# A transformer layer on one core: attention's high parts move from VectorE to ScalarE and GpSimd, and the fixed SBUF places move to a top on 128 bytes

## The chip, the cores and the metric

The kernel runs on one core of a Trainium2 chip. The metric is the device time of one launch in microseconds. TensorE multiplies, VectorE (DVE), ScalarE (ACT) and GpSimd (POOL) do the element work, and SyncE (SP) issues most transfers.

## What is computed

One layer over 2048 frames of width 1024, in fp32:

```
h = x @ w_in                                   # one projection for both head groups
o_gdn = gated_delta_rule(...)                  # 4 heads, chunks of 64 frames
q_nope,q_rope = rms_norm(c_q) @ w_uq ; k_nope,v = rms_norm(c_kv) @ w_ukv ; rotary on q_rope, k_rope
for each block of queries, head by head:       # 4 heads, 128 + 64 wide, v 128 wide
    s = (q_nope k_nope^T + q_rope k_rope^T) * scale, later chunks masked
    o = softmax(s) v
x = layer_norm(alpha x + concat(o_gdn, o_mla) @ w_out)
x = layer_norm(alpha x + (silu(gate) * up) @ w_down)
out = x + sigmoid(x @ w_ple_gate) * (p @ w_ple)
```

## The kernel before

Every fp32 product is made of three matmuls in a fast fp32 format. An operand x is split into a high part (x rounded by a copy into that format) and a low part (x minus the high part), and low x high, high x low and high x high are added in PSUM. So every operand needs one copy and one subtraction before TensorE can use it.

The program is a row of stages: input projection (tiles in_), latents (lat_), delta rule (dr_), attention (at_), output projection with norm (op_), the feed-forward's first half (ff_), its second half with norm (fd_), and the embedding (em_). Each stage is one block of five engine programs that are written out in full; each engine runs its own in order, with semaphores between them, and a barrier of all engines stands between two stages. op, fd and em share one product routine (class TokenProduct, its matmuls at L2451 to L2453): the moving operand of a matmul is the weight (512 columns), the stationary one the activation (128 columns).

**Where tiles lie.** A Scope places a stage's tiles one behind the other from the first free byte of a partition, 16,512 (129 x 128); each start is rounded up to 32 bytes. An Early places tiles at a fixed distance below a top, so that a stage can load them while the stage before still runs. A partition's usable end is 229,368. All distances below the top are multiples of 128, so a fixed tile's remainder modulo 128 is that of the top. Before, the top is 229,344, with remainder 96. Fixed are: attention's inputs of head 0, which serve all even heads (q_hi0, q_lo0, k_hi0, k_lo0, v_hi0, v_lo0, qr0), the rotary keys of all heads (kr, kr_hi), the raw buffers of op, ff, fd and em, and the weights' high and low parts in fd and em. Placed by a Scope are attention's inputs of odd heads (remainder 0), its prob (0), pT_hi and pT_lo (64), op's weights and activations (both 32), fd's activations (32: an identity of 512 bytes and four small tiles, together 160 bytes, lie ahead of them) and em's activations (0).

**Attention.** Queries are cut into 8 blocks of 256 per head, in the order j = 7, 0, 6, 1, 5, 2, 4, 3; block j has j+1 pairs of key tiles, so a head has 36 pairs. For every pair TensorE transposes four 128x128 tiles of probabilities (L1702), ScalarE rounds them (pT_hi, L1751), VectorE subtracts (pT_lo, L1814), and TensorE multiplies them with v (L1716 to L1718). The tiles are turned two pairs ahead of their use (AHEAD = 2, three buffers). In the same pairs the scores of the block three places on are made: five matmuls for each group of 512 keys (L1685 to L1689), a row maximum on VectorE (L1782), an exp on ScalarE (L1738); at a block's end VectorE makes factors from maxima and sums (gap L1792, scale L1808) and GpSimd multiplies the probabilities by them (L1651). All of this is listed by one generator, steps(), and each engine walks the list in its own order.

**Pieces.** While head h is worked on, head h+1's q, k, rotary q and v are loaded and split, in 16 pieces of 512 columns (kind = m % 4: q, k, rotary q, v), spread over the pairs 2 to 20 of the head. Head 3 has no next head and no pieces. SyncE loads a piece into one of four raw slots (`load`, L1856 to L1861), as soon as the low part of the piece four before it is done. VectorE makes the high part (split_highs: L1828, and L1825 and L1826 for rotary q) behind the maxima of that pair. GpSimd makes the low part (`low`: L1662, L1659) and counts split_low.

**Start.** GpSimd clears an identity and writes its diagonal. TensorE waits for it before its first score, though only the transposes read it.

Of the kernel before, what the change touches and what calls it, by code (L numbers as in the profile page):

```python
# [28 lines left out]
P = 128  # L29
# [55 lines left out]
class Early:  # L85
# [4 lines left out]
        self.nc, self.stage, self.sems = nc, stage, []  # L90

    def sb(self, name, shape, below_top, dt=F32):
        top = self.nc.sbuf_usable_end // 32 * 32
        return self.nc.alloc_sbuf_tensor_at(f"{self.stage}_{name}", shape, dt, offset=top - below_top)

    def sem(self, name):
# [59 lines left out]
def reached(eng, sem, count):  # L156

    if not (isinstance(count, int) and count <= 0):
        eng.wait_ge(sem, count)
# [1378 lines left out]
def attention(nc, made, mixT, at, op, w_out, mixed):  # L1538
# [20 lines left out]
    with ExitStack() as ctx:  # L1559
# [6 lines left out]
        ident = s.sb("ident", [P, P])  # L1566
        raw = s.sb("raw", [P, RAW, NTOK])
        qr_hi = s.sb("qr_hi", [P, NTOK], F32R)
        prob = [s.sb(f"prob{n}", [P, 2, (SEQ, SEQ // 2)[n % 2]]) for n in range(4)]
        negm = s.sb("negm", [P, 4, 2, 4])  # L1570
        sums = s.sb("sums", [P, 4, 2, 4])
# [12 lines left out]

        const_sem = s.sem("consts")
        raw_loaded = [s.sem(f"raw_loaded{n}") for n in range(RAW)]
        split_high, split_low = s.sem("split_high"), s.sem("split_low")
        score_done = s.sem("score_done")
        diag_done = s.sem("diag_done")
        max_done = s.sem("max_done")  # L1590
# [48 lines left out]
        @block.gpsimd  # L1639
        def _(pool):  # L1640
            def scaling(n):
                pool.wait_ge(scale_done, n + 1)
                g, ops = groups[n], []
                for tile in range(2):
                    if g > 1:
                        view = keys_of(n, tile, 0, NTOK * (g - 1)).rearrange("p (g n) -> p g n", n=NTOK)
                        ops.append((view, scale[:, n % 4, tile, 0:g - 1].unsqueeze(2).broadcast_to([P, g - 1, NTOK])))
                    w = widths(blocks[n][1], tile)[-1]
                    ops.append((keys_of(n, tile, g - 1, w), scale[:, n % 4, tile, g - 1:g].broadcast_to([P, w])))
                for view, by in ops:  # L1650
                    last = pool.tensor_tensor(view, view, by, ALU.mult)  # L1651
                last.then_inc(scaled, 1)

            def low(h, m):
                count, slot, kind, ts = piece(h, m)
                b, src = h % 2, raw[:, slot]
                pool.wait_ge(split_high, count + 1)
                if kind == 2:
                    pool.tensor_tensor(qr[b][0:ROPE, ts], src[0:ROPE], qr_hi[0:ROPE].bitcast(F32), ALU.subtract).then_inc(split_low, 1)  # L1659
                else:  # L1660
                    high, to = ((q_hi, q_lo), (k_hi, k_lo), None, (v_hi, v_lo))[kind]
                    pool.tensor_tensor(to[b][:, ts], src, high[b][:, ts].bitcast(F32), ALU.subtract).then_inc(split_low, 1)  # L1662

            pool.memset(ident[:], 0.0).then_inc(const_sem, 1)
            pool.wait_ge(const_sem, 1)
            pool.affine_select(out=ident[:], in_=ident[:], compare_op=ALU.not_equal, fill=1.0, base=0, pattern=[[-1, P]],
                               channel_multiplier=1).then_inc(const_sem, 1)
            for n in range(LOOK):
                scaling(n)
            for n, p, turns, now, ends, whole, left, pieces in steps():  # L1670
                if whole is not None:
                    scaling(whole)
                for h, m in pieces:
                    low(h, m)

        @block.tensor
        def _(pe):
# [12 lines left out]

            def turn(n, p):
                j, k = blocks[n][1], pair0[n] + p
                if p == 0:
                    pe.wait_ge(scaled, n + 1)
                reached(pe, lo_done, k + 1 - T_RING)
                for kt in range(2):
                    for tile in range(2):
                        if p == j and kt > tile:
                            continue
                        to = QB * kt + P * (tile if p < j or kt == 0 else 0)  # L1700
                        src = prob[n % 4][:, tile, P * (2 * p + kt):P * (2 * p + kt) + P]
                        last = pe.transpose(pT_ps[:, k % T_RING, to:to + P], src, ident[:])  # L1702
                last.then_inc(turned, 1)
# [14 lines left out]
                    last = pe.matmul(acc, v_hi[b][:, vs], pT_hi[:, r, ps], start=False, stop=diag)  # L1718
                last.then_inc(pv_done, 1)

            pe.wait_ge(const_sem, 2)
            for n in range(LOOK):
                for group in score_groups(n):
                    scores(*group)
# [8 lines left out]
        def _(act):  # L1733
            def exps(n, tile, g, w, G, _):
                if tile == 0 and g == 0 and n >= 4:
                    act.wait_ge(turned, pair0[n - 3])
                act.wait_ge(max_done, G + 1)
                act.activation(keys_of(n, tile, g, w), score_ps[:, G % S_RING, 0:w], ACT.Exp,  # L1738
                               bias=negm[:, n % 4, tile, g:g + 1], accum_out=sums[:, n % 4, tile, g:g + 1]).then_inc(exp_done, 1)
# [13 lines left out]
            def out_copy(n):  # L1753
                act.wait_ge(pv_done, pair0[n + 1])
                reached(act, stored[n % 2], 16 * (n // 2))
                act.activation(out[:, n % 2], acc_ps[:, n % ACCS, 0:QB], ACT.Copy).then_inc(out_done, 1)

            act.preload_act_table(ACT.Exp)
            for n in range(LOOK):
                for group in score_groups(n):  # L1760
# [2 lines left out]
            for n, p, turns, now, ends, whole, left, pieces in steps():  # L1763
                if left is not None:
                    out_copy(left)
                for n1, p1 in turns:
                    high(n1, p1)
                for group in now:
                    exps(*group)
                if ends is not None:  # L1770
                    factors(ends)
            out_copy(N - 1)
# [2 lines left out]
        def _(dve):  # L1775
# [38 lines left out]
                dve.tensor_tensor(pT_lo[:, r, 0:w], pT_ps[:, r, 0:w], pT_hi[:, r, 0:w].bitcast(F32),  # L1814
                                  ALU.subtract).then_inc(lo_done, 1)

            def split_highs(h, m):
                count, slot, kind, ts = piece(h, m)
                b, src = h % 2, raw[:, slot]
                if h > 1 and m == 0:  # L1820
                    dve.wait_ge(pv_done, pair0[NB * (h - 1)])
                dve.wait_ge(raw_loaded[slot], sum(32 if j % 4 == 2 else 16 for j in range(slot, count + 1, RAW)))
                if kind == 2:
                    reached(dve, split_low, count + 1 - 4)
                    dve.tensor_copy(qr_hi[:], src)  # L1825
                    dve.tensor_copy(qr[b][ROPE:, ts], src[ROPE:]).then_inc(split_high, 1)  # L1826
                else:
                    dve.tensor_copy((q_hi, k_hi, None, v_hi)[kind][b][:, ts], src).then_inc(split_high, 1)  # L1828

            for n in range(LOOK):  # L1830
                for group in score_groups(n):
                    maximum(*group)
# [2 lines left out]
            for n, p, turns, now, ends, whole, left, pieces in steps():  # L1835
                for n1, p1 in turns:
                    low(n1, p1)
                if whole is not None:
                    scales(whole)
                for group in now:  # L1840
                    maximum(*group)
                for h, m in pieces:
                    split_highs(h, m)
                if ends is not None:
                    gaps(ends)

# [1022 lines left out]
```

## Time and profile before

| | |
|---|---|
| median of 3 timed runs | 3357.72 us (3351.21 to 3359.09) |
| the profiled execution | 3339.58 us, span 3338.0 us |
| mean granted TensorE clock | 0.965 |
| TensorE matmuls busy | 3081.1 us, 92% |
| VectorE, ScalarE, GpSimd busy | 1648.7, 1056.6, 1057.2 us |
| attention, first score to last matmul | 1061.8 to 1459.1 us |

A matmul is pipelined: its shown length overlaps the next one's. The pace of a stream is the distance from one start to the next. The clock column of the windows is a share of the full 2.4 GHz; the granted clock has the two levels 1.2 and 2.4 GHz, so 0.88 means that 24% of the stretch ran at 1.2 GHz.

### The profile page before, as it was taken

The page shows a single profiled execution, that of the slowest core. Times are in us where ns is not written, and L with a number is a line of the kernel's source. Part 1 is how long each engine was busy: PE and PEld are TensorE (multiplying, and loading weights), DVE is VectorE, ACT ScalarE, POOL GpSimd, SP SyncE. Part 2 cuts the span into 40 slices and gives each one's busy share as a digit, 9 for nine tenths or more (in the row PEclk, how much of TensorE's full clock was granted, in tenths as well). Part 3 has the DMA queues.
Part 4 walks back from the last instruction along what each step waited for, and adds up shares of the span by engine and source line. Part 5 has one row for each costly group of instructions (what it writes and reads, how often), then busy time and mean ns, then how long its engine had stood idle before and what let it go on. Part 6 is the DMA issues. An engine that isn't in the chain of part 4 may idle for free. (4 is left out here: it accounts for less than half of the span.)

```text
span 3338.0 us, 44243 instructions
## 1 busy us (share of the span) xinstructions
PE 3081.1 (92%) x15074; PEld 2541.3 (76%) x15074; DVE 1648.7 (49%) x2773; ACT 1056.6 (32%) x2363; POOL 1057.2 (32%) x1184
## 2 busy tenths in 40 slices
PE   7999997869997889989979999899998999999898
PEld 5888885658886777878758888788887788887776
DVE  3654004536665777656585555865555433233433
ACT  2111014335554444542243333433333211111321
POOL 2322241066665555410073333543331000000122
PEclk9999998979998989999989999999999999999999
DMA  3211115422324211125723222232223433233433
GB/s 137 87 75 75 75 57 183 143 75 75 82 63 106 61 50 54 67 76 181 239 69 115 94 75 80 71 117 94 76 79 111 136 97 96 90 96 122 148 121 99
DMA packets 284412, 329.17 MB, mean 99 GB/s; under 512 B 33280, under 2 KB 224640, under 8 KB 279936
## 3 DMA queue, kind: packets, MB, share of 16 engines
q1 hardware_dynamic: 238632, 265.84, 25.0%
q0 software_dynamic: 12384, 45.09, 3.8%
q10 hardware_dynamic: 33280, 16.78, 1.8%
q8 instruction: 62, 1.02, 0.1%
q14 instruction: 54, 0.44, 0.0%
HBM read 210.73 MB, written 116.92 MB: 98 GB/s over the span
## 5 line engine op out<-in xcount | busy, mean ns | idle before, releaser
L2061 PE MATMUL ff_bank<-ff_x_hi,ff_w_lo 128*128 128x512 f32 x1240 | 488.3, 394 | 32.8 <-DVE ff_w_lo L2241 22.0
L2062 PE MATMUL ff_bank<-ff_x_lo,ff_w_hi 128*128 128x512 f32 x1240 | 487.4, 393 | 0.0
L2063 PE MATMUL ff_bank<-ff_x_hi,ff_w_hi 128*128 128x512 f32 x1240 | 486.9, 393 | 0.0
L2044 POOL TENSOR_TENSOR ff_w_sum<-ff_w_raw 128x512 f32<-128x512 f32 x210 | 299.6, 1436 | 496.9 <-DVE ff_w_lo L2241 438.0
L2061 PEld LDWEIGHTS ff_bank<-ff_x_hi,ff_w_lo 128*128 128x128 f32 x1240 | 235.7, 190 | 85.2 <-DVE ff_w_lo L2241 25.0
L296 PE MATMUL in_h_ps<-in_x_hi,in_w_lo 128*128 128x512 f32 x704 | 276.6, 393 | 25.0 <-POOL in_w_lo L252 25.0
L2451 PE MATMUL fd_acc<-fd_w_hi,fd_a_lo 128*128 128x512 f32 x704 | 280.1, 398 | 10.8 <-DVE fd_a_lo L2435 10.7
L2452 PE MATMUL fd_acc<-fd_w_lo,fd_a_hi 128*128 128x512 f32 x704 | 278.3, 395 | 0.0
L2453 PE MATMUL fd_acc<-fd_w_hi,fd_a_hi 128*128 128x512 f32 x704 | 278.1, 395 | 0.0
L297 PE MATMUL in_h_ps<-in_x_lo,in_w_hi 128*128 128x512 f32 x704 | 276.1, 392 | 0.0
L298 PE MATMUL in_h_ps<-in_x_hi,in_w_hi 128*128 128x512 f32 x704 | 276.0, 392 | 0.0
L2063 PEld LDWEIGHTS ff_bank<-ff_x_hi,ff_w_hi 128*128 128x128 f32 x1240 | 235.8, 190 | 49.7
L2062 PEld LDWEIGHTS ff_bank<-ff_x_lo,ff_w_hi 128*128 128x128 f32 x1240 | 235.8, 190 | 49.0
L2140 ACT ACTIVATE ff_w_hi<-ff_w_sum 128x512 fp32r<-128x512 f32 x210 | 132.5, 631 | 288.3 <-PE ff_bank L2063 267.1
L2435 DVE TENSOR_TENSOR fd_a_lo<-fd_a_raw,fd_a_hi 128x256 fp32r<-128x256 f32 x176 | 74.5, 423 | 286.2 <-ACT fd_a_hi L2425 286.2
L2425 ACT ACTIVATE fd_a_hi<-fd_a_raw 128x256 fp32r<-128x256 f32 x176 | 73.4, 417 | 361.4 <-PE fd_acc L2453 356.5
L1651 POOL TENSOR_TENSOR at_prob<-at_prob,at_scale 128x1536 f32<-128x1536 f32 (+4 forms) x112 | 137.8, 1261 | 149.3 <-DVE at_scale L1808 141.1
L296 PEld LDWEIGHTS in_h_ps<-in_x_hi,in_w_lo 128*128 128x128 f32 x704 | 133.4, 189 | 53.8 <-issue 16.8
L2530 POOL DMA_DIRECT2D scratch_x<-fd_w_raw x16 | 8.5, 534 | 511.8 <-DVE fd_w_raw L2631 511.8
L2451 PEld LDWEIGHTS fd_acc<-fd_w_hi,fd_a_lo 128*128 128x128 f32 x704 | 132.2, 188 | 45.1 <-DVE fd_w_lo L2432 10.8
L2453 PEld LDWEIGHTS fd_acc<-fd_w_hi,fd_a_hi 128*128 128x128 f32 x704 | 132.2, 188 | 32.7
L2452 PEld LDWEIGHTS fd_acc<-fd_w_lo,fd_a_hi 128*128 128x128 f32 x704 | 132.3, 188 | 31.4
(380 smaller groups left out, 6582.6 us busy)
## 6 DMA issues: line engine op xcount, KB each, us to landing
ff_w_raw<-w_gate_up SPq DMA_DIRECT2D x44, 1024.0 KB, 5.1
scratch_hT<-in_out SPq DMA_DIRECT2D x22, 1024.0 KB, 3.9
fd_a_raw<-scratch_hid SPq DMA_DIRECT2D x176, 128.0 KB, 2.1
dr_qkv<-scratch_hT SPq DMA_DIRECT2D x16, 768.0 KB, 5.1
in_w_raw<-w_in POOLq DMA_DIRECT2D x22, 512.0 KB, 3.9
scratch_hid<-ff_first SPq DMA_DIRECT2D x44, 256.0 KB, 2.3
scratch_hid<-ff_second SPq DMA_DIRECT2D x44, 256.0 KB, 2.3
fd_w_raw<-w_down SPq DMA_DIRECT2D x22, 512.0 KB, 5.3
```

Source lines behind the costliest of these rows:

```text
L296: pe.matmul(acc, w_lo[:, b, ws], x_hi[:, k, ts], start=(k == 0), stop=False)
L297: pe.matmul(acc, w_hi[:, b, ws], x_lo[:, k, ts], start=False, stop=False)
L298: last = pe.matmul(acc, w_hi[:, b, ws], x_hi[:, k, ts], start=False, stop=(k == KD - 1))
L1651: last = pool.tensor_tensor(view, view, by, ALU.mult)
L2044: pool.tensor_tensor(w_sum[:, SUM_SLOT[m]], w_raw[:, b, one], w_raw[:, b, two], op).then_inc(w_sum_done, 1)
L2061: pe.matmul(acc, w_lo[:, wm, ws], x_hi[:, xm, k], start=first_mm, stop=False, skip_group_check=skip)
L2062: pe.matmul(acc, w_hi[:, wm, ws], x_lo[:, xm, k], start=False, stop=False, skip_group_check=skip)
L2063: return pe.matmul(acc, w_hi[:, wm, ws], x_hi[:, xm, k], start=False, stop=last_mm, skip_group_check=skip)
L2140: act.activation(w_hi[:, m], src, ACT.Copy).then_inc(w_hi_done, 1)
L2451: pe.matmul(to, self.a_lo[:, slot, rows], self.w_hi[:, k, cols], start=(k == k0), stop=False)
L2452: pe.matmul(to, self.a_hi[:, slot, rows], self.w_lo[:, k, cols], start=False, stop=False)
L2453: last = pe.matmul(to, self.a_hi[:, slot, rows], self.w_hi[:, k, cols], start=False, stop=(k == k1))
```

## The change

- The top from which the fixed places are counted becomes a multiple of 128: 229,248, 96 bytes lower.
- Attention's high parts of q and rotary q are made by ScalarE (split_high, behind the exps of the pair), those of k and v by GpSimd as src + 0, in `low` itself, ahead of the subtraction. VectorE makes none. The semaphore split_high becomes act_high and pool_high. Both engines now wait for the raw slot themselves.
- A new tile zero (128 x 1) holds the 0; it lies ahead of prob and moves prob and all behind it by 32 bytes.
- TensorE waits for the identity at its first turn instead of ahead of the first score.

```diff
-        top = self.nc.sbuf_usable_end // 32 * 32
+        top = self.nc.sbuf_usable_end // P * P
...
+        zero = s.sb("zero", [P, 1])
...
-        split_high, split_low = s.sem("split_high"), s.sem("split_low")
+        act_high, pool_high, split_low = s.sem("act_high"), s.sem("pool_high"), s.sem("split_low")
...
-                pool.wait_ge(split_high, count + 1)
+                if kind % 2 == 0:
+                    pool.wait_ge(act_high, count // 2 + 1)
+                else:
+                    if h > 1 and m == 1:
+                        pool.wait_ge(pv_done, pair0[NB * (h - 1)])
+                    pool.wait_ge(raw_loaded[slot], sum(32 if j % 4 == 2 else 16 for j in range(slot, count + 1, RAW)))
+                    high = (k_hi if kind == 1 else v_hi)[b]
+                    pool.tensor_tensor(high[:, ts], src, zero[:, 0:1].broadcast_to([P, NTOK]), ALU.add).then_inc(pool_high, 1)
+                    pool.wait_ge(pool_high, count // 2 + 1)
...
-            pool.wait_ge(const_sem, 1)
+            pool.memset(zero[:], 0.0).then_inc(const_sem, 1)
+            pool.wait_ge(const_sem, 2)
...
+                if k == 0:
+                    pe.wait_ge(const_sem, 3)
...
-            pe.wait_ge(const_sem, 2)
...
+            def split_high(h, m):
...
+                count, slot, kind, ts = piece(h, m)
+                b, src = h % 2, raw[:, slot]
+                if h > 1 and m == 0:
+                    act.wait_ge(pv_done, pair0[NB * (h - 1)])
+                act.wait_ge(raw_loaded[slot], sum(32 if j % 4 == 2 else 16 for j in range(slot, count + 1, RAW)))
+                if kind == 2:
+                    reached(act, split_low, count + 1 - 4)
+                    act.activation(qr_hi[:], src, ACT.Copy)
+                    act.activation(qr[b][ROPE:, ts], src[ROPE:], ACT.Copy).then_inc(act_high, 1)
+                else:
+                    act.activation(q_hi[b][:, ts], src, ACT.Copy).then_inc(act_high, 1)
...
                 for group in now:
                     exps(*group)
+                for h, m in pieces:
+                    if m % 2 == 0:
+                        split_high(h, m)
```

VectorE's split_highs and its call behind the maxima are removed.

## Rows read from the trace of the kernel before

**Rows 1.** The page: TensorE's busy time and those of the others

```profile
PE 3081.1 (92%) x15074; PEld 2541.3 (76%) x15074; DVE 1648.7 (49%) x2773; ACT 1056.6 (32%) x2363; POOL 1057.2 (32%) x1184
```

**Rows 2.** Windows: blocks j=7 to j=5 of heads 0 to 3; busy us (instructions), clock, DMA

```profile
1087.40:1151.20 63.80, 55.54 (x343) 49.29 (x344) 49.08 (x93) 27.12 (x72) 41.66 (x34) 0.92 0.22 62
1185.00:1254.50 69.50, 58.77 (x348) 51.41 (x345) 53.57 (x101) 29.23 (x79) 42.59 (x34) 0.88 0.20 59
1288.00:1356.70 68.70, 57.37 (x345) 50.41 (x344) 53.63 (x101) 28.92 (x79) 42.45 (x34) 0.90 0.19 56
1390.50:1444.80 54.30, 51.00 (x348) 45.51 (x346) 31.82 (x81) 28.51 (x79) 21.37 (x18) 1.00 0.26 95
```

**Rows 3.** Windows: blocks j=7 and j=6 of head 1, then of head 3

```profile
1185.00:1203.50 18.50, 14.27 (x92) 12.63 (x89) 15.17 (x26) 6.18 (x16) 11.94 (x8) 0.82 0.20 57
1211.70:1229.80 18.10, 15.01 (x92) 13.45 (x89) 15.83 (x25) 6.66 (x19) 12.77 (x10) 0.81 0.25 72
...
1390.50:1403.50 13.00, 11.84 (x90) 10.75 (x89) 7.36 (x20) 6.29 (x16) 6.38 (x4) 1.00 0.03 11
1412.10:1424.30 12.20, 11.48 (x92) 10.70 (x90) 7.03 (x18) 6.45 (x19) 5.53 (x4) 1.00 0.63 247
```

**Rows 4.** Groups by form, VectorE, heads 0 to 2: busy us, mean ns | idle before

```profile
L1828 DVE CAST at_k_hi<-at_raw 128x512 fp32r<-128x512 f32 x12 | 13.6, 1136 | 0.0
...
L1825 DVE CAST at_qr_hi<-at_raw 128x512 fp32r<-128x512 f32 x12 | 8.8, 734 | 0.0
L1792 DVE TENSOR_TENSOR at_gap<-at_top,at_negm 128x6 f32<-128x6 f32 x6 | 7.7, 1281 | 0.2
```

**Rows 5.** Tile at_raw: one reader, duration ns min/median/max

```profile
L1828 DVE CAST at_k_hi<-at_raw x12: 416/598/2119, 1094.2 to 1348.5; 128x512 fp32r<-128x512 f32 x12
```

**Rows 6.** Timeline of VectorE, GpSimd and TensorE in block j=6 of head 0

```profile
1113.65 2.02 DVE L1826 CAST at_qr<-at_raw 64x512 fp32r<-64x512 f32 x1
...
1113.38 6.01 POOL L1651 TENSOR_TENSOR at_prob<-at_prob,at_scale 128x1024 f32<-128x1024 f32 x4 [2.49 <-DVE at_scale L1808]
...
1116.45 0.39 PE L1716 MATMUL at_acc_ps<-at_pT_hi,at_v_lo 128*128 128x256 f32 x1 [2.35 <-DVE at_pT_lo L1814]
```

**Rows 7.** Groups by form: a ScalarE copy from SBUF, GpSimd's product and subtraction

```profile
L1343 ACT ACTIVATE at_k_hi<-dr_sq 128x512 fp32r<-128x512 f32 x1 | 0.6, 632 | 0.0
...
L1651 POOL TENSOR_TENSOR at_prob<-at_prob,at_scale 128x512 f32<-128x512 f32 x32 | 33.6, 1056 | 33.8 <-DVE at_scale L1808 33.8
L1662 POOL TENSOR_TENSOR at_k_lo<-at_raw,at_k_hi 128x512 fp32r<-128x512 f32 x12 | 15.7, 1310 | 15.4 <-DVE at_k_hi L1828 15.4
```

**Rows 8.** DMA issues in heads 0 to 2: a q piece, KB, us to landing

```profile
at_raw<-scratch_qnT SPq DMA_DIRECT2D x11, 256.0 KB, 3.1
```

**Rows 9.** Timeline at attention's start: GpSimd and TensorE

```profile
1061.11 0.21 POOL L1664 MEMSET at_ident<- 128x128 f32 x1 [1.17 <-POOLq L82]
...
1061.82 0.79 PE L1685 MATMUL at_score_ps<-at_k_hi,at_q_lo 128*128 128x512 f32 x1 [5.33 <-POOL at_ident L1666]
```

**Rows 10.** Timeline: first and last of 33 (op), 25 (fd), 17 (em) matmuls

```profile
1519.71 0.39 PE L2451 MATMUL op_acc<-op_w_hi,op_a_lo 128*128 128x512 f32 x1
...
1526.97 0.39 PE L2453 MATMUL op_acc<-op_w_hi,op_a_hi 128*128 128x512 f32 x1
...
2799.80 0.39 PE L2451 MATMUL fd_acc<-fd_w_hi,fd_a_lo 128*128 128x512 f32 x1
...
2805.40 0.39 PE L2451 MATMUL fd_acc<-fd_w_hi,fd_a_lo 128*128 128x512 f32 x1
...
3199.81 0.40 PE L2452 MATMUL em_gate_ps<-em_w_lo,em_a_hi 128*128 128x512 f32 x1
...
3203.55 0.39 PE L2453 MATMUL em_gate_ps<-em_w_hi,em_a_hi 128*128 128x512 f32 x1
```

**Rows 11.** Tiles: the transposes of op and of fd, ns min/median/max

```profile
L2552 PE MATMUL op_xT_ps<-op_ident,op_y x128: 270/272/473, 1494.6 to 1667.5; 128*128 128x128 f32 x128
...
L2552 PE MATMUL fd_xT_ps<-fd_ident,fd_w_raw x128: 270/273/475, 2633.5 to 3085.0; 128*128 128x128 f32 x128
```

More of the change, by code:

```diff
@@ L1815, in low @@
                                   ALU.subtract).then_inc(lo_done, 1)
[L1817 to L1828, printed above, removed]
             for n in range(LOOK):
@@ L1841, in _ @@
                     maximum(*group)
-                for h, m in pieces:
-                    split_highs(h, m)
                 if ends is not None:
```

## The prediction

> **What bounds the kernel now.** I read the page first: TensorE is busy in 92% of the span, no other engine above half [rows 1]. So a gain must come either from gaps of TensorE or from the pace of its matmuls. The change touches both: the work that it moves lies in attention, and the addresses that it moves are read by matmuls in four stages.
>
> *Attention, by windows.* Every head runs the same 36 pairs of key tiles in the same order. Heads 0, 1 and 2 split the next head's inputs into high and low parts during their pairs 2 to 20; head 3 has nothing to split. The first five blocks (24 pairs, 343 to 348 matmuls in every head) take 63.8, 69.5 and 68.7 us in heads 0 to 2 and 54.3 us in head 3 [rows 2]. The reader should look at the matmul counts (equal), at VectorE (49 to 54 us busy against 32) and at the granted clock: 0.92, 0.88 and 0.90 against 1.00. At levels of 2.4 and 1.2 GHz that is (0.08 x 63.8 + 0.12 x 69.5 + 0.10 x 68.7) x 2 = 41 us at 1.2 GHz, which loses 20 us; the other 19 us of the difference are gaps. Within a head the loss sits in the two long blocks, j=7 and j=6: 18.5 and 18.1 us in head 1, 13.0 and 12.2 us in head 3 [rows 3].
>
> *Why.* A VectorE copy of 128x512 takes 0.42 us at best; its mean is 0.7 to 1.1 us, its longest 2.12 us [rows 4, 5]. The timeline shows it stretched to 2.02 us at 1113.65, next to GpSimd's row of four products from 1113.38 to 1119.39. The pT_lo behind it is late, and TensorE waits 2.35 us for pT_lo [rows 6]. So a copy on VectorE waits for a running GpSimd instruction, and the values' matmul waits behind the copy. The Trainium skill, SBUF — State Buffer, "Who interferes with whom", names this: fp32 copies in VectorE's two-port mode and GpSimd exclude each other for a whole instruction. The stretched copies agree.
>
> **The change, part by part.**
>
> *Removed.* 60 VectorE copies, 56.8 us (five groups of twelve: 13.6+12.1+11.4+10.9+8.8, the first and last in [rows 4]). If nothing took their place, heads 0 to 2 would run at head 3's pace: 63.8+69.5+68.7 - 3 x 54.3 = 39.1 us. That is the ceiling of this part.
>
> *Added on ScalarE.* Per head 4 q_hi, 4 qr_hi and 4 upper qr: 12 x 0.63 = 7.6 us [rows 7]. ScalarE is busy 28.5 of head 3's 54.3 us [rows 2], so there is room on average. But two of three such pieces put 1.26 us ahead of the next pT_hi; tiles are turned two pairs ahead of their use (some 3 us), so I take it as covered.
>
> *Added on GpSimd.* 8 high parts a head; src plus a broadcast column is nearest to the 128x512 product with a broadcast scale, 1.06 us, so 8.5 us a head (bounds 1.0 and 1.3 us, between that and the subtraction, 1.31) [rows 7]. GpSimd then has 21.4 (head 3, products alone) + 16 x 1.29 + 8.5 = 50.5 us of work in 54.3 us [rows 2]: it fits over the head, not in each block. In block j=6: 5.5 us of products, 6 lows, 3 highs = 16.4 us against 12.2 us [rows 3]. It ends some 4 us late and catches up in the block after. What is late next is the raw ring: the load for piece m+4 is issued only when low(m) is done and lands 3.1 us later [rows 8]. ScalarE, in order, waits for it ahead of its exps and pT_hi. With products that start 3 us into block 6, low(6) ends near 10.4 us, piece 10 lands at 13.5 us, and its place in the queue comes at 9 to 11 us: about 3 us of waiting. Two pairs of turned tiles cover about half. I charge 1.0 us in block 7 of heads 1 and 2, 1.5 us in each block 6 and 0.8 us in the two blocks behind: 2.3+3.3+3.3 = 8.9 us. Of the 20 us lost to clock I let 4 remain (a stall or two). So this part gives 39.1 - 8.9 - 4 = 26.2 us. Bounds: 8 us (the pieces' waits hardly shorter than now) and 39.1.
>
> VectorE keeps tensor_tensor instructions with two operands in SBUF. One of them, the gap (128x6), has a mean of 1281 ns in heads 0 to 2 [rows 4], as long as one GpSimd subtraction. With GpSimd busier these wait as now or more, up to one 2.7 us product; this is in the 8.9.
>
> *The identity.* TensorE's first score waits until 1061.82 for an identity that only the transposes read; GpSimd, free of the barrier, starts at 1061.11 [rows 9]. Gain 0.7 us. The new memset delays the identity by 0.1 us, hidden by 22 us of scores.
>
> *The addresses.* Usable end 229,368: the top goes from 229,344 (96 past a multiple of 128) to 229,248 (0 past). What the trace says about such remainders: the same product line runs its 512-column matmuls at (1526.97 - 1519.71)/32 = 226.9 ns in op, where weights and activations both lie 32 past; at (2805.40 - 2799.80)/24 = 233.3 ns in fd, weights 96 past, activations 32; and at (3203.55 - 3199.81)/16 = 233.8 ns in em, 96 and 0 [rows 10]. All three runs are at full clock and without a gap. I read this as: equal remainders are fast, unequal ones cost 6.6 ns a matmul, and the 32 itself costs nothing (op). After the change em has 0 and 0: 960 x 6.6 ns = 6.3 us, TensorE being the bound there. fd has 0 and 32: unequal still, at em's old distance (32 below the weights' multiple, as 96 and 0 are), so em's price, which is fd's own within the 0.5 ns that the reading allows: 0. Bounds for fd: the whole step of 6.6 ns is given back, 2112 x 6.6 = 13.9 us faster, or a second step comes on top, as much slower. fd would pass any gain on, for TensorE runs there from one matmul to the next. Heads 1 and 3 (q and k at 0, kr at 96) become equal: 400 score matmuls x 3 ns = 1.2 us. The new tile zero shifts prob and pT by 32: pT to 96 against v at 0, unequal before (64 against 96 or 0) and after, 0. For prob the transposes of op (equal) and fd (unequal) both have a median of 272 or 273 ns [rows 11]: 0.
>
> The Trainium skill, SBUF — State Buffer, "SBUF: two separate sides", says that outside the pair shared by VectorE and GpSimd the engines' ports never wait on anyone, TensorE's included; "Operand start alignment" asks only for a multiple of the element size and says its runs timed nothing. By that the move of the places would be worth 0 in em; it is a rival below, and the pace of the three streams [rows 10] speaks against it.
>
> *Sum.* 26.2 + 0.7 + 1.2 + 6.3 = 34.4 us. The profiled execution took 3339.6 us (span 3338.0), so 3305.2; the three timed runs have a median of 3357.7, 18 us higher, and the same subtraction gives 3323.3. I predict 3323.
>
> **Rivals.**
>
> *GpSimd becomes attention's bound (0.17).* Its 50.5 us of 54.3 leave no slack, and the ring makes ScalarE wait for it. The clock drops stay. Attention gives 8 us, the whole 16: 3342. For it: 16.4 us of work in a 12.2 us block. Against: products are needed five or more pairs after they are queued.
>
> *Addresses do nothing (0.13).* em stays at 233.8 ns, heads 1 and 3 too: 34.4 - 7.5 = 26.9, 3331. For it: the stages differ in more than remainders. Against: the same line, clock and shapes.
>
> *fd gains too (0.10).* The remainder of the weights alone decides below 64, or 32 is near enough: 34.4 + 13.9 = 48.3, 3309. Against: em's 233.8 ns at that same distance, and op.
>
> *Slower: ScalarE stands still for raw pieces (0.04).* Each of the 24 ScalarE pieces waits in full for a landing that GpSimd's lag has delayed. The waitless gain is 39.1+0.7+1.2+6.3 = 47.3 us, so it decides from 47.3/24 = 2.0 us of uncovered wait a piece on; at the full 3.1 us the kernel loses 27 us: 3385. Against: half the pieces find their slot loaded long before.
>
> *The forecast has 0.55*; 0.01 is left for no effect.
>
> **Numbers.** 0.3% (10 us) is about what a measurement here can tell from no change. Faster by more: forecast, addresses-do-nothing, fd, and two thirds of GpSimd's rival, 0.90; within: 0.06; slower: 0.04. Range: down to 3298 (ceiling of attention and em, half of fd), up to 3344 (attention at its lower bound, em gaining).
>
> **What would show it.** Right: no copies on VectorE; the three stretches at 57 to 61 us with the clock at 0.96 or more; em at 227 ns; fd still near 233; the first score at 1061.1. Wrong: ScalarE rows that wait for DMA at_raw for over 2 us, GpSimd without gaps in blocks 7 and 6 followed by TensorE waits for at_scale or pT_lo, the clock still under 0.92, or fd at 227 or 238 ns.

## The result and the profile after

The changed kernel takes 3328.85 us (median of 7 runs, 3322.99 to 3333.30); the kernel before, timed beside it, takes 3351.21 us (7 runs, 3343.42 to 3359.09). The ratio is 0.9933, 95% interval 0.9919 to 0.9947: 22.4 us less, where the sum said 34.4. The profiled executions are closer to each other than the medians: 3339.6 us before (below its seven timed runs), 3328.9 us after. The stages, each from the start of its first matmul to that of its last, and the change's gain in each:

| stage (us) | in | lat | dr | at (attention) | op | ff | fd | em |
|---|---|---|---|---|---|---|---|---|
| before | 493.0 | 129.5 | 390.0 | 397.3 | 199.2 | 879.2 | 516.3 | 229.3 |
| after | 495.2 | 129.8 | 396.5 | 384.3 | 199.0 | 877.5 | 516.8 | 225.6 |
| gain | -2.2 | -0.3 | -6.5 | 13.0 | 0.2 | 1.7 | -0.5 | 3.7 |

The page of the profile after, the line of busy times. VectorE has lost 55 us and 60 instructions against [rows 1], ScalarE and GpSimd have gained 19 and 21 us:

```profile
PE 3072.8 (92%) x15074; PEld 2540.9 (76%) x15074; DVE 1593.7 (48%) x2713; ACT 1075.9 (32%) x2399; POOL 1077.9 (32%) x1209
```

The windows of the first five blocks of heads 0 to 3, after (columns as in [rows 2]):

```profile
1096.70:1158.50 61.80, 53.35 (x343) 47.23 (x344) 32.02 (x73) 33.95 (x84) 47.48 (x41) 0.94 0.23 65
1192.30:1256.60 64.30, 54.95 (x347) 48.29 (x345) 33.49 (x82) 36.22 (x91) 49.53 (x42) 0.92 0.25 69
1289.50:1352.80 63.30, 54.14 (x347) 47.67 (x345) 33.02 (x81) 36.11 (x91) 48.16 (x41) 0.95 0.21 61
1386.40:1440.70 54.30, 51.06 (x347) 45.72 (x346) 31.74 (x81) 28.64 (x79) 21.38 (x18) 1.00 0.26 95
```

VectorE's busy time in heads 0 to 2 is now head 3's (32 to 33 us), but the blocks are not as short: 61.8 + 64.3 + 63.3 = 189.4 us against 202.0 in [rows 2], 12.6 us less, where the forecast had 26.2 and no stretch longer than 61. The clock is 0.92 to 0.95, not 0.96 and more. Where the rest sits is seen block by block. Windows of head 1's blocks j=7, j=6 and j=1, and of head 3's j=1:

```profile
1192.20:1205.20 13.00, 11.90 (x91) 10.83 (x90) 7.47 (x20) 7.96 (x19) 9.05 (x7) 1.00 0.05 17
1214.50:1227.20 12.70, 11.76 (x90) 10.76 (x89) 7.07 (x18) 8.01 (x21) 9.25 (x8) 1.00 0.17 40
1227.20:1241.80 14.60, 10.43 (x52) 8.64 (x51) 7.25 (x17) 6.34 (x17) 10.31 (x11) 0.77 0.43 119
1428.90:1437.90 9.00, 8.84 (x64) 8.12 (x63) 4.98 (x16) 5.34 (x17) 4.67 (x4) 1.00 0.04 15
```

The two long blocks are cured: 13.0 and 12.7 us at full clock, against 18.5 and 18.1 in [rows 3], and 13.0 and 12.2 in head 3. The short block j=1 is not: 14.6 us at a clock of 0.77 (15.2 and 15.5 in heads 0 and 2) where head 3 takes 9.0, and where before it was 11.8, 11.8 and 13.0. So some 6 us a head are lost there.

The groups by form behind this: ScalarE's three kinds of copies, GpSimd's high part, and VectorE's gap in heads 0 to 2, in two sizes.

```profile
L1781 ACT ACTIVATE at_q_hi<-at_raw 128x512 fp32r<-128x512 f32 x12 | 7.6, 631 | 0.2 <-DMA at_raw<-scratch_qnT 0.2
L1778 ACT ACTIVATE at_qr_hi<-at_raw 128x512 fp32r<-128x512 f32 x12 | 7.6, 630 | 4.2 <-DMA at_raw<-scratch_qrT 4.2
L1779 ACT ACTIVATE at_qr<-at_raw 64x512 fp32r<-64x512 f32 x12 | 7.5, 628 | 0.1
...
L1665 POOL TENSOR_TENSOR at_k_hi<-at_raw,at_zero 128x512 fp32r<-128x512 f32 x12 | 12.5, 1040 | 0.0
...
L1820 DVE TENSOR_TENSOR at_gap<-at_top,at_negm 128x4 f32<-128x4 f32 x6 | 2.3, 384 | 0.2
L1820 DVE TENSOR_TENSOR at_gap<-at_top,at_negm 128x6 f32<-128x6 f32 x6 | 1.0, 166 | 0.2
```

The prices were right (0.63 us and 1.04 us, [rows 7] gave 0.63 and 1.06). ScalarE's wait for the loads is 4.4 us in all, three of them long. The timeline of block j=1 of head 1, ScalarE, then VectorE, then TensorE, shows what one such wait sets off:

```profile
1228.67 0.63 ACT L1778 ACTIVATE at_qr_hi<-at_raw 128x512 fp32r<-128x512 f32 x1 [1.49 <-DMA at_raw<-scratch_qrT]
1229.32 0.63 ACT L1779 ACTIVATE at_qr<-at_raw 64x512 fp32r<-64x512 f32 x1
1229.97 0.49 ACT L1762 ACTIVATE at_pT_hi<-at_pT_ps 128x384 fp32r<-128x384 f32 x1
1231.66 0.47 ACT L1749 ACTIVATE at_prob<-at_score_ps,at_negm 128x256 f32<-128x256 f32 x1 [1.20 <-DVE at_negm L1810]
...
1230.49 0.56 DVE L1842 TENSOR_TENSOR at_pT_lo<-at_pT_ps,at_pT_hi 128x384 fp32r<-128x384 f32 x1 [4.12 <-ACT at_pT_hi L1762]
1231.05 0.11 DVE L1808 MEMSET at_score_ps<- 64x64 f32 x1
1231.20 0.42 DVE L1810 TENSOR_REDUCE at_negm<-at_score_ps 128x1 f32<-128x256 f32 x1
...
1234.02 0.71 DVE L1829 TENSOR_TENSOR at_part<-at_fac,at_sums 128x4 f32<-128x4 f32 x1
...
1235.23 1.28 DVE L1810 TENSOR_REDUCE at_negm<-at_score_ps 128x1 f32<-128x512 f32 x2
...
1232.28 0.33 PE L1695 MATMUL at_score_ps<-at_k_hi,at_q_lo 128*128 128x128 f32 x1 [1.77 <-ACT at_prob L1749]
...
1236.84 0.79 PE L1695 MATMUL at_score_ps<-at_k_hi,at_q_lo 128*128 128x512 f32 x1 [2.39 <-ACT at_prob L1749]
1237.43 0.63 PE L1696 MATMUL at_score_ps<-at_kr,at_qr 128*128 128x512 f32 x1
1237.86 0.63 PE L1697 MATMUL at_score_ps<-at_kr_hi,at_qr 128*128 128x512 f32 x1
```

The reader should follow one piece, the rotary q piece (it takes two copies). ScalarE stands 1.49 us for its load, copies twice 0.63 us, and only then makes pT_hi at 1229.97. VectorE has stood 4.12 us by then, 2.8 of them through this piece's load and copies; its queue has pT_lo first and the maximum of the next scores behind it, so the maximum comes at 1231.20, the exps of those scores at 1231.66, and a score buffer comes free for TensorE at 1232.28, after 1.77 us of waiting. Four microseconds on TensorE waits again, 2.39 us, but no copy of a piece stands in ScalarE's queue there. The exp that it waits for (1236.01) waits for the maxima of 1235.23, and in VectorE's queue these stand behind the block's end: pT_lo, then the products of the factors. One of them, part (128x4), takes 0.71 us, where it takes 0.15 in head 3. By then the granted clock is at its lower level: the score matmuls start 0.43 us apart (1237.43, 1237.86) instead of 0.23.

The other two parts. At attention's start the first score waits for nothing but the barrier, 4.66 us where it was 5.33 for the identity [rows 9], and in em matmuls are at (3306.22 - 3301.01)/23 = 226.5 ns (233.8 in [rows 10]):

```profile
1070.63 0.77 PE L1695 MATMUL at_score_ps<-at_k_hi,at_q_lo 128*128 128x512 f32 x1 [4.66 <-PEq L82]
...
3301.01 0.39 PE L2464 MATMUL em_gate_ps<-em_w_hi,em_a_lo 128*128 128x512 f32 x1
...
3306.22 0.39 PE L2466 MATMUL em_gate_ps<-em_w_hi,em_a_hi 128*128 128x512 f32 x1
```

### The profile page after: what moved, and what is told of

It reads as the page before. It is cut to its first block and busy times, and to the rows that moved or that the text cites. A ratio compares the mean times of both kernels' runs of the same rounds, so it can differ in the third digit from the quotient of the medians.

```text
span 3327.4 us, 44247 instructions
## 1 busy us (share of the span) xinstructions
PE 3072.8 (92%) x15074; PEld 2540.9 (76%) x15074; DVE 1593.7 (48%) x2713; ACT 1075.9 (32%) x2399; POOL 1077.9 (32%) x1209
## 3 DMA queue, kind: packets, MB, share of 16 engines
q1 hardware_dynamic: 238632, 265.84, 25.1%
## 5 line engine op out<-in xcount | busy, mean ns | idle before, releaser
L2464 PE MATMUL fd_acc<-fd_w_hi,fd_a_lo 128*128 128x512 f32 x704 | 279.2, 397 | 11.5 <-DVE fd_a_lo L2448 11.5
L2464 PEld LDWEIGHTS fd_acc<-fd_w_hi,fd_a_lo 128*128 128x128 f32 x704 | 132.6, 188 | 44.6 <-DVE fd_w_lo L2445 10.7
```

The costliest lines, as they stand in the source:

```text
L2464: pe.matmul(to, self.a_lo[:, slot, rows], self.w_hi[:, k, cols], start=(k == k0), stop=False)
```

## Experiments

Each ratio is against the kernel before, timed beside it. The line numbers of a kernel are its own.

**The change in two halves.** First the places alone, then the change with the old places and the identity awaited at the start as before.

```diff
 e1_places (before.py)
-        top = self.nc.sbuf_usable_end // 32 * 32
+        top = self.nc.sbuf_usable_end // P * P
 e2_pieces (after.py)
-        top = self.nc.sbuf_usable_end // P * P
+        top = self.nc.sbuf_usable_end // 32 * 32
...
-                if k == 0:
-                    pe.wait_ge(const_sem, 3)
...
+            pe.wait_ge(const_sem, 3)
             for n in range(LOOK):
```

> The kernel before with the top on 128 bytes alone. Theory (equal remainders of weights and activations are fast): the embedding's 512-column matmuls go from 233 to 227 ns, fd's stay near 233 (0 against 32), attention keeps its VectorE copies and its clock drops; 6 to 8 us less than before. Rival (addresses do nothing, the embedding got faster for another reason): 0 us, the embedding at 233 ns.

> The changed kernel with the old top and the old wait for the identity: what is left is the work moved from VectorE to ScalarE and GpSimd. Theory: attention's first five blocks of heads 0 to 2 take 12 to 14 us less together than before, the embedding stays at 233 ns; 13 to 16 us less than before in all. Rival (most of the gain lies in the places): under 8 us.

Measured: e1 3343.5 us, ratio 0.9994 (0.9981 to 1.0008); e2 3332.9 us, ratio 0.9965 (0.9951 to 0.9978), with 3347.6 before. In e1 em takes 227.3 us (229.3 before), its 512-column matmuls stand 227.5 ns apart; fd's spacing stays at 233.3. The gain of 2 us is in the trace; the ratio, whose interval ends at 6 us less, shows none of the 6 to 8 expected. The profiled execution spent 412.1 us in dr. In e2 attention takes 384.9 us and the five blocks 63.4, 63.6 and 64.7 us: the pieces alone make nearly all of attention's gain (12.4 of 13.0 us; in the five blocks 10.3, where 12 to 14 were expected).

**Six raw buffers instead of four**, against the theory that the raw ring makes block j=1's loss.

```diff
-    RAW = 4
+    RAW = 6
```

> The changed kernel with six raw slots instead of four. Theory (ScalarE waits for piece 10's raw slot, since its load is issued only when GpSimd's late low part of piece 6 is done): ScalarE's wait for the DMA goes, the block j=1 falls from 15 us to 9 to 11 us in heads 0 to 2, the clock drops of heads 1 and 2 go; 10 to 17 us less than the changed kernel. Rival (the 1.26 us of copies in ScalarE's queue ahead of the next pT_hi, and GpSimd's load, cause the stall by themselves): under 4 us.

Measured: 3328.4 us, ratio 0.9950 (0.9935 to 0.9966). ScalarE's wait for the loads is gone, and attention takes 381.9 us, 2.4 less. But j=1 is still at 13.9, 14.4 and 14.0 us. Without the load's wait j=1 is about 1 us shorter; the rest needs another cause. The rival came out, not the theory.

**Who makes the high parts.** All by GpSimd (ScalarE has none), then all by ScalarE (GpSimd has none).

```diff
 e6_pool_all
-                if kind % 2 == 0:
-                    pool.wait_ge(act_high, count // 2 + 1)
...
+                    high = (q_hi, k_hi, None, v_hi)[kind][b]
+                    pool.tensor_tensor(high[:, ts], src, zero[:, 0:1].broadcast_to([P, NTOK]), ALU.add).then_inc(pool_high, 1)
 e7_act_all
+                pool.wait_ge(act_high, count + 1)
...
-                    if m % 2 == 0:
-                        split_high(h, m)
+                    split_high(h, m)
```

> The change with every high part on GpSimd and none on ScalarE: ScalarE has 7.5 us a head less, GpSimd 10.4 us a head more. Theory that ScalarE's copies ahead of its exps and pT_hi make the 5 to 6 us that the small block j=1 loses in each of three heads: block j=1 falls from 15 to 9 to 12 us and the time lies at or below that of the change, 3315 to 3328. Rival, that GpSimd's load (its products and its high and low parts) makes it: block j=1 stays or grows and the next head's pieces come late, 3335 to 3370.

> The change with every high part on ScalarE and none on GpSimd: ScalarE has 5.0 us a head more, GpSimd 8.3 us a head less. Theory that ScalarE's queue makes block j=1's loss: it stays or grows, and the blocks j=6 and j=5 as well, 3332 to 3345 us. Rival, GpSimd's load: block j=1 falls towards 9 to 12 us, 3315 to 3325.

Measured: e6 3337.6 us, ratio 0.9989 (0.9971 to 1.0007); e7 3333.3 us, 0.9966 (0.9950 to 0.9981). With no copies on ScalarE block j=1 falls to 10.3, 11.7 and 10.1 us and the five blocks of heads 0 to 2 to 54.8, 59.4 and 57.1 us, 18 us below the change. With all on ScalarE j=1 is at 13.6, 14.8 and 13.7 us (after: 15.2, 14.6 and 15.5) and j=6 goes from 12.7 to 13.8. So ScalarE's copies are the larger part of j=1's loss; but j=1 didn't grow with more of them, and it got 1.6 and 1.8 us shorter in heads 0 and 2, so they aren't all of it. Yet e6 is slower than the change, and the waits of TensorE in attention say why: time in all, times, longest.

```profile
PE at_score_ps L1698 <- POOL at_v_lo L1674: 24.3, 3, 9.2
PE at_acc_ps L1731 <- DVE at_pT_lo L1844: 14.5, 22, 1.7
PE at_score_ps L1698 <- ACT at_prob L1752: 9.6, 10, 2.1
```

Once a head, in block j=2, TensorE asks for the first score of the next head, and GpSimd has not finished that head's pieces: 7 to 9 us each, 24.3 in all. My expectation for e6 had missed this: the pieces' own deadline, which the change itself meets within 1.2 us in all.

**The pieces at other pairs**, none at or next to the two pairs of block j=1.

```diff
-    FIRST_PIECE, PIECE_STEPS = 2, 20
+    PIECE_AT = (1, 2, 3, 4, 6, 7, 9, 10, 11, 12, 13, 14, 19, 20, 21, 22)
```

> The change with the sixteen pieces at other pairs of a head: at pairs 1 to 4, 6, 7, 9 to 14 and 19 to 22, so that none stands at the two pairs of block j=1 (16 and 17) nor next to them. If the pieces that stand there make its loss, whoever makes them, block j=1 falls from 15 to 9 to 12 us and the blocks j=6 and j=5 change by less than 2 us: 3313 to 3322 us. If the loss is only moved with the pieces (their load is the same), block j=6 or j=5 gains what j=1 loses, and the time stays within 3 us of the change's 3328.

Measured: 3342.9 us, ratio 0.9994 (0.9977 to 1.0010). Block j=1 falls to 10.5 to 10.7 us, but j=6, with six pieces in a row, goes to 16.9, j=0 to 12.6 in two heads and j=2 to 16.8: attention 398.3 us. (In j=6 is a wait of 3.9 us for pT_lo, the last thing before the first values' matmul of j=1.) The loss goes where pieces stand close, so it is theirs; it isn't only moved, as the rival had it, but grows, for the time lies some 20 us above the change's by the two ratios.

**The three late even pieces elsewhere**: pieces 10, 12 and 14 (two of them rotary, with two copies) made by VectorE (in `late`, the same copies as in split_high), or by GpSimd in `low`; ScalarE keeps the five early ones. Both have the padding of the next group. The last kernel is e10 with six raw buffers.

```diff
 e10_late_dve, e11_late_pool
-                    if m % 2 == 0:
+                    if m % 2 == 0 and m < LATE:
                         split_high(h, m)
...
 e10_late_dve, in VectorE's loop behind the maxima
+                for h, m in pieces:
+                    if m % 2 == 0 and m >= LATE:
+                        late(h, m)
 e12_late_dve_ring6 (e10_late_dve)
-    RAW = 4
+    RAW = 6
```

> The change with the padding of 96 bytes in the down-projection, and with the high parts of the even pieces from the tenth on (three of eight a head: ten, twelve and fourteen) given back to VectorE; ScalarE keeps the five early ones, GpSimd the odd ones. If ScalarE's late copies make block j=1's loss, it falls from 15 to 10 to 12 us, block j=6 stays at 12.7, the hand-over block j=2 at 13.4: 8 to 12 us less than the change with the padding, 3309 to 3315 us. Rival, that VectorE's copies are stretched beside GpSimd's work and hold pT_lo as long: j=1 stays above 13 and the time at 3319 to 3325.

> The same, but the three late even pieces' high parts are made by GpSimd (5.2 us a head more there, where all eight cost 10.4 more). If block j=1's loss is ScalarE's, it falls to 10 to 12 us; GpSimd's backlog at the hand-over (9.6 us in block j=2 with all eight) is about half, 2 to 5 us: 3312 to 3319 us. Rival, that all of the backlog comes from the late pieces: j=2 at 18 us or more, 3322 to 3330.

> The change with the padding of 96 bytes, the three late even pieces' high parts on VectorE, and six raw buffers instead of four. In the run before it with four buffers VectorE stood 2.4 us for the tenth piece's load, ScalarE's exps then 5.1 us for its maximum, and block j=1 stayed at 15.3 to 15.6. If block j=1's loss is the load's wait in front of whatever queue makes pT's parts, plus ScalarE's copies, both are gone here and it falls to 10 to 12 us (with six buffers and ScalarE's copies it was 13.9 to 14.4), the hand-over block j=2 returns from 16 to 13.4: 3308 to 3315 us. Rival, that VectorE's copies, stretched beside GpSimd's work, cost pT_lo what ScalarE's cost pT_hi: j=1 at 13 to 15 us and 3315 to 3321 us, no better than the change with the padding alone.

Measured: e10 3322.8 us, ratio 0.9925 (0.9900 to 0.9951); e11 3318.4 us, 0.9899 (0.9877 to 0.9921); e12 3315.9 us, 0.9907 (0.9888 to 0.9925). Head 1's blocks, in the order in which they run:

| us | j=7 | j=0 | j=6 | j=1 | j=5 | j=2 | attention |
|---|---|---|---|---|---|---|---|
| before | 18.5 | 8.2 | 18.1 | 11.8 | 12.9 | 13.3 | 397.3 |
| after | 13.0 | 9.3 | 12.7 | 14.6 | 14.7 | 12.6 | 384.3 |
| e3, six buffers | 13.0 | 9.0 | 12.8 | 14.4 | 14.7 | 12.4 | 381.9 |
| e6, all GpSimd | 13.0 | 8.5 | 12.9 | 11.7 | 13.3 | 22.1 | 394.8 |
| e11, late ones GpSimd | 13.0 | 9.3 | 12.7 | 12.8 | 11.4 | 19.5 | 388.2 |
| e10, late ones VectorE | 13.0 | 9.1 | 12.7 | 15.6 | 12.8 | 14.7 | 390.4 |
| e12, the same, six buffers | 13.0 | 9.0 | 12.7 | 15.2 | 12.7 | 16.2 | 390.5 |
| head 3, no pieces | 13.0 | 8.5 | 12.2 | 9.0 | 11.5 | | |

In heads 0 and 2 block j=2 of e10 takes 16.3 us, not 14.7. GpSimd relieves j=1 and j=5 (5 us together) and gives it back at the hand-over, so its rival (18 us and more in j=2) came out there, though the time lies where the theory had it. VectorE doesn't relieve j=1 at all, with four buffers or six; its copies of the rotary piece in e12's timeline, ahead of pT_lo:

```profile
1225.70 1.53 DVE L1857 CAST at_qr_hi<-at_raw 128x512 fp32r<-128x512 f32 x1
1227.25 1.42 DVE L1858 CAST at_qr<-at_raw 64x512 fp32r<-64x512 f32 x1
1228.70 0.56 DVE L1846 TENSOR_TENSOR at_pT_lo<-at_pT_ps,at_pT_hi 128x384 fp32r<-128x384 f32 x1
```

2.95 us for two copies, of which one takes 0.42 us at its shortest [rows 5], while GpSimd subtracts beside them; ScalarE needs 1.26 us. So e12's rival, not its theory, came out: the rotary piece costs time ahead of pT's parts on either engine that makes them.

It isn't the only cost in j=1. Here are TensorE's waits within the block (those over 0.15 us), and VectorE's three small instructions with two operands in SBUF that stand ahead of its maxima (gap, part and scale, 128x4), both from the traces:

| j=1, heads 0, 1, 2 | TensorE waits, us | gap + part + scale, us | block, us |
|---|---|---|---|
| head 3, after | 0.8 | 0.5 | 9.0 |
| before | 2.0, 2.0, 3.1 | 1.6, 1.6, 1.6 | 11.8, 11.8, 13.0 |
| e6, all GpSimd | 2.1, 1.9, 1.9 | 1.8, 1.7, 1.7 | 10.3, 11.7, 10.1 |
| e11, late ones GpSimd | 2.7, 3.0, 2.7 | 2.3, 2.3, 2.3 | 12.5, 12.8, 12.5 |
| e7, all ScalarE | 3.6, 3.6, 3.7 | 0.5, 0.5, 0.5 | 13.6, 14.8, 13.7 |
| e3, six buffers | 3.9, 3.7, 3.9 | 2.4, 2.4, 2.4 | 13.9, 14.4, 14.0 |
| after | 4.4, 4.2, 4.4 | 1.5, 1.4, 1.5 | 15.2, 14.6, 15.5 |
| e12, late ones VectorE | 4.2, 4.5, 4.2 | 2.4, 2.4, 2.4 | 15.0, 15.2, 15.0 |

In e7 the three take as long as in head 3, and TensorE still waits 2.8 us more than there: that is ScalarE's queue alone. In e6 no copy stands ahead of pT's parts, and TensorE waits 1.1 to 1.3 us more than in head 3, as the three take 1.2 to 1.3 us more: that is the share of VectorE's small instructions, stretched while GpSimd works. e3 took the load's wait away, but the three then took 0.9 to 1.0 us more than in the change, which ate part of it; e12 has both costs. The two shares are read from these pairs of traces; no run changes the three instructions alone. e10 to e12 can't be told from one another by their ratios, and their attention is longer than the change's.

**The places.** Where activations and weights of the product start was moved by padding: 96 bytes in fd on the change (e4); on the kernel before, with the old top, 64 bytes in fd and 96 in em (e5), and 192 in fd and 96 in em (e9).

```diff
         root = s.sb("root", [P, 4])
+        if stage == "fd":
+            s.sb("pad", [P, 24])        # e4 (e5: 16, e9: 48)
...
         y = s.sb("y", [P, 2, D_MODEL])
+        s.sb("pad", [P, 24])            # e5 and e9
```

> The changed kernel with 96 unused bytes ahead of fd's activations, so that they have remainder 0 as fd's weights have. Theory (equal remainders): fd's matmuls go from 233 to 227 ns, 2112 x 6.6 ns = 14 us less than the changed kernel. Rival (fd is slow for another reason: the place of its weights, its transfers, its 22 tiles): 0 us, still 233 ns.

> The kernel before (top counted on 32 bytes) with 64 bytes of padding in the down-projection and 96 in the last stage, so that there weights and activations both start at remainder 96 of 128 bytes. Theory that equal remainders decide: matmuls of 512 columns at 227 ns in both stages instead of 233 (fd about 506 us instead of 517, em 226 instead of 229), 3333 to 3337 us, ratio 0.995 to 0.997. Rival, that a multiple of 128 bytes is needed: both stay at 233 ns and the ratio at 1.000. It also looks at the wait of some 3 us in the stage of down-rotations near its 150th us, which the four runs with the new top had and the two with the old top had not: if the top sets it, it is absent here; if it falls by chance, it may be here.

> The kernel before (old top) with 192 bytes of padding in the down-projection and 96 in the last stage: the activations' start minus the weights' start is then a multiple of 256 bytes in both. In the runs so far the matmul's pace went with that difference modulo 256: 0 gave 227 ns; 64 (the down-projection before) 233.3; 160 (the same after, the last stage before) 231 to 238 in turns; 128 (the down-projection with 64 bytes of padding) 228 to 241. Theory, equal modulo 256: both stages at 227 ns, the down-projection's stage 506 us (516 before), ratio 0.996 to 0.997. Rival, that it needs the new top: the down-projection stays at 231 to 235 ns and the ratio at 0.999.

Measured: e4 3321.2 us, ratio 0.9916 (0.9897 to 0.9936); e5 3339.7 us, 0.9988 (0.9976 to 0.9999); e9 3325.6 us, 0.9929 (0.9909 to 0.9948). By the medians the padding alone, with nothing else of the change (e9), gives as much as the whole change; by the stages it is less, 10.7 us in fd and 2.6 in em, and the rest of its 25.1 us isn't in any stage that the padding touches (15.5 us separate the two profiled executions). Timelines, the first and the last of 131 matmuls of fd and of 24 of em: of e5,

```profile
2986.79 0.39 PE L2452 MATMUL fd_acc<-fd_w_lo,fd_a_hi 128*128 128x512 f32 x1
...
3017.00 0.39 PE L2453 MATMUL fd_acc<-fd_w_hi,fd_a_hi 128*128 128x512 f32 x1
...
3298.40 0.39 PE L2451 MATMUL em_gate_ps<-em_w_hi,em_a_lo 128*128 128x512 f32 x1
...
3303.61 0.39 PE L2453 MATMUL em_gate_ps<-em_w_hi,em_a_hi 128*128 128x512 f32 x1
```

and of e9, fd:

```profile
2972.77 0.40 PE L2452 MATMUL fd_acc<-fd_w_lo,fd_a_hi 128*128 128x512 f32 x1
...
3002.24 0.39 PE L2453 MATMUL fd_acc<-fd_w_hi,fd_a_hi 128*128 128x512 f32 x1
```

(3017.00 - 2986.79)/130 = 232.4 ns in fd of e5, though both operands lie 96 past a multiple of 128 there, and 5.21/23 = 226.5 ns in em; 29.47/130 = 226.7 ns in fd of e9. What orders all of them is the start of the activations (stationary) minus that of the weights (moving), modulo 256 bytes. By the layout told above the fixed tiles are at 224 with the old top and at 128 with the new one (their distances are multiples of 1024), and a Scope begins at 128:

| difference mod 256 | where | spacing of 512-column matmuls |
|---|---|---|
| 0 | op; em after, e5, e9; fd in e4, e9 | 227 ns |
| 64 | fd before, e2 | 233.3, even |
| 128 | fd in e5 | 232.4; single ones 228 to 241 |
| 160 | em before; fd after, e1 | 231 to 238 in turns, mean 233.3 |

Attention holds a second test that nobody set up. In heads 1 and 3 two of the five score matmuls read q-side tiles of a Scope against kr and kr_hi below the top: a difference of 160 with the old top, 0 with the new one; in heads 0 and 2 it is 0 with both. Score matmuls of 512 columns that follow each other within 250 ns are 232.0 to 232.5 ns apart on average in heads 1 and 3 of the four kernels with the old top (before, e2, e5, e9) and 229.4 to 230.1 in the ten with the new one; heads 0 and 2 have 229.4 to 230.2 in all fourteen. So 0 doesn't give 227 everywhere, in these short rows it gives 229 to 230. In long rows it does: the in and ff stages, whose tiles all start at equal remainders of 256, have 226.6 to 227.0. The latents' v, with 64, has 233.2.

## Why the prediction was right in sign and place, and too high in its sum

*The number.* 3323 was forecast and 3328.9 measured, and part of that nearness is luck: the gain was 12.0 us too high (34.4 against 22.4), and the time of the kernel before, from which it was taken off, was 6.5 us too high (3357.7 from three runs, 3351.2 from seven).

*Attention's pieces, 26.2 us: mis-sized, 12.6 measured.* The ceiling of 39.1 us and what was removed stand: the long blocks came down to head 3's lengths, as forecast. What failed is the step that took ScalarE's 1.26 us ahead of pT_hi "as covered" because tiles are turned two pairs ahead, and the 8.9 us of waits that were placed in blocks 7 and 6. Those blocks show none. Block j=1 shows 5.6 to 6.5 us a head over head 3 (18.3 us in all; it was 9.6 before), j=5 another 1.5 to 3.2. The covered distance is two pairs, and in j=1 it does cover the values' matmuls, which wait for nothing; it doesn't cover what stands behind pT_lo in VectorE's queue, the maximum, from which exps, score buffers and TensorE's next scores hang. I had asked only who waits for pT. That ScalarE's queue is the larger share is shown by e6 and e7; that the load's wait is a small one by e3; that the rotary piece costs as much on VectorE by e10 and e12. The other share, VectorE's small instructions ahead of the maxima, the prediction had put with the 8.9 us of blocks 7 and 6; it came in j=1.

*The clock.* 41.0 us at half clock in the five blocks of heads 0 to 2 became 23.9, so 8.5 of the 20 us came back, not 16: 20.5 us of the 23.9 lie in block j=1 with its stalls, and the clocks of the blocks are 0.92, 0.88 and 0.90 in [rows 2] and 0.94, 0.92 and 0.95 in the windows above.

*The gap.* I had it wait as now or more (1281 ns, [rows 4]). It fell to 166 ns for 128x6, with GpSimd busier than before. But part for 128x4 rose from 0.15 to 0.70 us in j=1; gap, part and scale of the five blocks of heads 0 to 2 together fell from 18.1 to 11.1 us. They take 8.1 us in e7 and 20.9 in e6. So GpSimd's busy time alone doesn't tell it; that it depends on what GpSimd runs at the moment when one of them comes is likely, but nothing was run to show it.

*Identity, 0.7 us: right* (5.33 - 4.66 = 0.67).

*em, 6.3 us: the pace right, the stage 3.7.* Matmuls closer than 250 ns apart have a mean of 233.4 ns before and 227.2 after: 920 x 6.2 = 5.7 us. What the longer steps between them, at tile changes and at the stage's slow start, take beyond 227 ns each is 5.7 us before and 7.8 after: 2.1 us of the gain became waiting. TensorE isn't the bound at every tile change, as I had assumed.

*fd, nothing: right, by a reading that was too coarse.* fd's mean stayed at 233.3 ns (516.3 and 516.8 us). But "equal remainders of 128 are fast" would have given fd of e5 227 ns; the period that fits all runs is 256. The rival "addresses do nothing" fell: e4 and e9 move nothing but places in fd and gain 10.3 and 10.7 us in it (13.5 by the pace; some 3 us became longer steps, as in em). The Trainium skill, SBUF — State Buffer, "SBUF: two separate sides", which stood beside that rival, says that TensorE's ports never wait on anyone. These runs don't test that; they show that the pace depends on places all the same.

*Scores and transposes.* The 1.2 us of heads 1 and 3 is too small to be found in blocks of 54.3 us (head 3 took 54.3 before and after), but the spacing shows it: 232.2 ns before and 229.5 after, by my estimate about 1 us over 400 score matmuls.

*The rest.* 13.0 + 0.7 + 3.7 = 17.4 us are accounted for (the 1.2 of the scores is in the 13.0), the medians differ by 22.4 with an interval of about 18 to 27. dr was 6.5 us longer in the profile after. I had first put that on the new top, since four kernels with it showed a longer wait for a load some 150 us into dr and two with the old top did not. That theory fell: e5 has the old top, the wait, and 396.1 us in dr, and e6 to e8 have the new top and 393.3 to 393.6. Over all fourteen profiles dr runs from 389.8 to 412.1 us with unchanged code, so it belongs to the execution, not to the change. Most of the difference goes with the clock: dr less half of its time at the lower clock (48.7 us of it before, 61.9 after, 84.4 in e1) is 365.5 to 367.4 us in thirteen of the profiles and 369.9 in e1. What sets the clock there is not settled.

*Of the rivals*, "GpSimd becomes the bound" gave 8 us in attention, and the 13.0 measured lies nearer to that than to 26.2. Its mechanism isn't what the trace shows: in the change TensorE's waits for GpSimd sum to 1.8 us, the longest 0.6, and ScalarE's for the ring to 4.4; with all pieces on GpSimd they are long (e6). "ScalarE stands still" has its mechanism, but 4.4 us of waits where it counted 24 x 3.1 = 74.

**The best version.** The fastest are e4, e10, e11 and e12 at 3316 to 3323 us; their intervals overlap. e4 is the simplest: the change and 96 bytes of padding in fd, 0.9916 (0.9897 to 0.9936) of the kernel before, with fd at 506.5 us and attention as in the change (384.4). It is faster than the kernel before by 26.4 us (3347.6 beside it), and against the change its gain is fd's 10.3 us in the trace.

## What to carry to other kernels

When work moves to another engine's queue, price it there, and ask not only who waits for the instruction behind it, but what is queued behind that waiter on its own engine: here the distance of two pairs covered the matmuls and not the maximum behind pT_lo. Head 3's blocks gave the ceiling; the short block, where least work stands between two deadlines, was where it wasn't reached, so look at the shortest block first. And look there at the small instructions too: three of 0.16 us took up to 2.4 us together beside GpSimd. Compare where an operand pair starts before anything else in a matmul-bound stage: 192 and 96 bytes of padding gave 13 us by the stages, as much as all the reworked split in attention.

## What the runs showed of the hardware

The spacing of fp32r matmuls of 512 columns at full clock goes with the start of the stationary operand (here the activations) minus that of the moving one (here the weights), modulo 256 bytes: in the long rows of op, fd and em 226.7 to 227.4 ns at 0, 232.4 to 233.4 at 64, 128 and 160; 10.7 us over fd's 2112 matmuls. Differences of 32, 96, 192 and 224 weren't tried, and what in the chip makes the difference isn't shown. VectorE's instructions of 0.16 us with two operands in SBUF took up to 1.30 us while GpSimd worked. And executions with the same code up to there can differ by 3 to 22 us in dr, most of it going with the granted clock.
